# Softmax one unit deeper in the attention slots, four gate chunks moved into slots 0 to 7, the weight fold cut into half-steps

## The reference

```python
def adaln_params(c, w, b):
    mod = jax.nn.silu(c) @ w + b            # shift, scale, gate
def attention_branch(h, ...):
    q, k, v, g = jnp.split(h @ w_in, ...)
    q = partial_rope(rms_norm(q, q_norm_g), positions)
    k = partial_rope(rms_norm(k, k_norm_g), positions)
    o = banded_sink_attention(q, k, v, sinks)   # window 128, softmax with a sink per head
    return (o * jax.nn.silu(g)) @ w_out
def pool_branch(h, ...):
    v, g = jnp.split(h @ w_in, [POOL_WIDTH], axis=-1)
    mixed = einsum('bsgc,gcd->bsgd', multiscale_pool(v), w_group) * scale
    return (mixed * jax.nn.silu(g)) @ w_out
for i in range(2):
    h = rms_norm(x, norm_g[i]) * (1.0 + scale) + shift
    x = x + gate * branch
```

## Time and profile before

| | before |
|---|---|
| median of 3 runs | 1516.83 us |
| the profiled execution | 1514.76 us |
| its span | 1513.0 us |
| PE busy | 1427.6 us, 94% of the span |
| PE's weight loads busy | 1206.2 us, 80% |
| DVE, ACT, POOL busy | 890.8, 537.3, 385.7 us |
| longest total wait of PE | 28.7 us, in the first stage |
| the next | 28.2 us in 16 waits, at_tr waiting for at_pr |

### The profile page before, as it was taken

How to read it: one execution, slowest core, us unless ns; L and a number is a source line. 1 busy time by engine, 2 the same in 40 slices (tenths; PEclk the granted TensorE clock), 3 DMA queues, 4 the chain that set the end, 5 groups by cost and what they waited for, 6 DMA issues and landing times.

```text
span 1513.0 us, 20206 instructions
## 1 busy us (share of the span) xinstructions
PE 1427.6 (94%) x7240; PEld 1206.2 (80%) x7240; DVE 890.8 (59%) x1524; ACT 537.3 (36%) x1270; POOL 385.7 (25%) x551
## 2 busy tenths in 40 slices
PE   1899999999999987799999999999999999999999
PEld 1678878788778876788888888788888888888887
DVE  7777666665444447777777775625555543555522
ACT  2443443333211126675555563322222212222200
POOL 2333333321222214455555554310000100000000
PEclk9999999999999998999999999999999999999999
DMA  8655555434899776756776765831121562112142
GB/s 311 219 183 194 192 186 199 176 138 169 336 345 366 282 296 229 252 216 217 287 274 236 283 256 202 299 98 54 45 76 49 169 193 72 47 42 77 50 153 84
DMA packets 96787, 285.62 MB, mean 189 GB/s; under 512 B 10768, under 2 KB 40496, under 8 KB 87088
## 3 DMA queue, kind: packets, MB, share of 16 engines
q1 hardware_dynamic: 87760, 250.74, 46.2%
q0 software_dynamic: 8928, 33.59, 6.4%
HBM read 196.22 MB, written 88.08 MB: 188 GB/s over the span
## 4 chain that ended last, share of the span: by engine, by line
PE 72%; DVE 9%; DMA 8%; ACT 5%; issue 3%; POOL 2%; SPq 1%; ACTq 0%; DVEq 0%; POOLq 0%
PE po_f_ps L1839 23%; PE po_y_ps L1855 12%; PE at_y_ps L1411 10%; PE ga_g_ps L929 8%; PE qk_proj L663 7%; PE at_o_ps L1395 5%; PE at_s_ps L1367 3%; DMA values_split<-qk_late 3%; DMA ga_ada<-in_ada_w 2%; PE at_tr L1377 2%; ACT at_pr L1187 1%; DMA ga_raw<-in_attn_w_gate 1%; DMA po_xn<-x_mid_t 1%; POOL qk_rq L306 1%; PE qk_tr L679 1%
## 5 line engine op out<-in xcount | busy, mean ns | idle before, releaser
L1839 PE MATMUL po_f_ps<-po_ht,po_w 128*128 128x512 f32 x1536 | 349.0, 389 | 0.0
L1839 PEld LDWEIGHTS po_f_ps<-po_ht,po_w 128*128 128x128 f32 x1536 | 288.2, 188 | 60.1 <-DVE po_ht L1701 0.3
L663 PE MATMUL qk_proj<-qk_w_qkv,qk_ht 128*128 128x512 f32 x1152 | 280.3, 399 | 7.0 <-DVE qk_w_qkv L539 4.0
L663 PEld LDWEIGHTS qk_proj<-qk_w_qkv,qk_ht 128*128 128x128 f32 x1152 | 214.9, 190 | 54.0 <-issue 6.1
L1411 PE MATMUL at_y_ps<-at_zt,at_w 128*128 128x512 f32 x768 | 198.4, 400 | 3.1 <-DVE at_x L1300 3.1
L1855 PE MATMUL po_y_ps<-po_zt,po_w 128*128 128x512 f32 x768 | 174.7, 389 | 0.0
L1855 PEld LDWEIGHTS po_y_ps<-po_zt,po_w 128*128 128x128 f32 x768 | 144.1, 188 | 29.9
L1411 PEld LDWEIGHTS at_y_ps<-at_zt,at_w 128*128 128x128 f32 x768 | 138.4, 190 | 28.7 <-issue 4.1
L1688 DVE TENSOR_TENSOR po_w<-po_raw,po_w 128x1024 fp32r<-128x1024 f32 x48 | 58.8, 1225 | 128.6 <-ACT po_w L1622 128.6
L1143 POOL TENSOR_SCALAR_AFFINE_SELECT at_pt<-at_ph 128x512 fp32r<-128x512 f32 x128 | 83.3, 674 | 188.6 <-ACT at_ph L1194 188.6
L306 POOL TENSOR_TENSOR qk_rq<-qk_mq,qk_half 128x8 f32<-128x8 f32 (+1 forms) x48 | 70.3, 1464 | 177.8 <-DVE qk_mq L485 177.7
(11 more groups left out here) (168 smaller groups left out, 1956.4 us busy)
## 6 DMA issues: line engine op xcount, KB each, us to landing
at_w<-out_weight_split SPq DMA_DIRECT2D x32, 1024.0 KB, 6.2
queries_t<-qk_late SPq DMA_DIRECT2D x16, 1024.0 KB, 4.0
ga_ada<-in_ada_w POOLq DMA_DIRECT2D x64, 256.0 KB, 4.9
at_qt<-queries_t SPq DMA_DIRECT2D x16, 1024.0 KB, 8.0
ht_split<-qk_ht SPq DMA_DIRECT2D x6, 2048.0 KB, 9.6
values_split<-qk_late SPq DMA_DIRECT2D x16, 768.0 KB, 4.5
at_vs<-values_split SPq DMA_DIRECT2D x16, 768.0 KB, 4.9
qk_late<-in_ada_w SPq DMA_DIRECT2D x16, 512.0 KB, 6.1
```

Source lines behind the costliest of these rows:

```text
L663: last = nc.tensor.matmul(proj[:, b * BANK:(b + 1) * BANK], ht[:, s % 2, m, k, t * P:(t + 1) * P], w_qkv[:, w, k, b * BANK:(b + 1) * BANK] ...
L1839: last = nc.tensor.matmul(f_ps[:, bank(j, h), :], w[:, i % 2, a, k, :], ht[:, h, m, k, :], start=(n == 0), stop=(n == 3 * KC - 1))
```

## The change

Three things are changed.

**Softmax one unit deeper.** In slot i PE now does p_round(i-2) and values(i-3), ACT does exps(i-1) ahead of `z_hi`, `p_hi(i-2)` comes behind it, and POOL masks unit i-2. `BEHIND` goes from 3 to 4, and the first output chunk from slot 19 to slot 20.

**Four gate chunks.** The dense part of the gate stage ends after 28 chunks. The last four (`FILL`) are done in slots 0 to 7 of the attention stage, 12 matmuls in each slot, on one PSUM bank (`FILL_BANK`); chunk n waits for the silu of chunk n-1. The last six pieces of the modulation sum move into slots 0 to 5, the last `sum_mods` to slot 7 and `set_mods` to slot 8. The pieces of the output weight begin at gate chunk 6 instead of 8.

**The fold.** It becomes 32 half-steps of 6 matmuls. Two go into each of the slots 9 to 19, behind the transposes; the other ten go in pairs into the second slot of output chunks 0 to 4. A half-step's load is 128 KB into one of two buffers, asked for one slot before ACT reads it. The folded pieces are evicted and stored singly.

```diff
@@ gate stage @@
+    FILL = KC // 2
+    DENSE = SLOTS - FILL
+    FIRST_BANKS, RING_BANKS, FILL_BANK = (6, 0, 1, 2), (6, 3, 4, 5), 6
     def g_bank(q):
-        return g_ps[:, (q + 2) % 4, :]
+        if q >= DENSE:
+            return g_ps[:, FILL_BANK, :]
+        return g_ps[:, FIRST_BANKS[q] if q < 4 else RING_BANKS[q % 4], :]
     def out_piece(q):
-        return (q - KC) // 3 if q >= KC and (q - KC) % 3 == 0 and (q - KC) // 3 < KC else None
+        return (q - 6) // 3 if q >= 6 and q % 3 == 0 and q < DENSE else None
+    def fill_product(pe, n, ks):
+        q, f = DENSE + n, FILL + n
+        if ks[0] == 0:
+            pe.wait_ge(silu_done, q if n > 0 else DENSE - 3)
+        for k in ks:
+            for w, m in PRODUCTS:
+                last = nc.tensor.matmul(g_bank(q), split_of(f, w)[:, k * P:(k + 1) * P], ht[(NSB - 2) % 2][:, m, k, :],
                                        start=(k == 0 and (w, m) == PRODUCTS[0]), stop=(k == KC - 1 and (w, m) == PRODUCTS[-1]))
...
@@ attention stage: places @@
-    BEHIND = 3
+    BEHIND = 4
+    FILL, FILL_SLOTS = ga["fill"], HALVES * ga["fill"]
+    FOLD_FROM = FILL_SLOTS + 1
+    def fold_slot(v):
+        return FOLD_FROM + v // 2 if v // 2 < EARLY else first_slot(v // 2 - EARLY) + HALVES - 1
+    def folds_in(i):
+        return [v for v in range(FOLDS) if fold_slot(v) == i]
...
@@ SP @@
-    def load_fold(sp, u):
-        wait(sp, fold_lo, u - 2)
-        sp.dma_start(wv_raw[:, u % 3], wvt[GC * f:GC * (f + 1)][:, :, pair * ROWS:(pair + 1) * ROWS].rearrange("c p n -> p c n")).then_inc(fold_loaded[u % 3], 16)
+    def load_fold(sp, v):
+        if v == 0:
+            sp.wait_ge(ga["g_done"], ga["slots"])
+            sp.wait_ge(weights["lo"], ga["items"])
+        if v >= 2:
+            sp.wait_ge(fold_lo, wv_split(v - 2))
+        sp.dma_start(wv_raw[:, v % 2], wvt[GC * f:GC * (f + 1)][:, :, b * P:(b + 1) * P].rearrange("c p n -> p c n")).then_inc(fold_loaded[v % 2], 16)
...
-            if i + 3 < FOLDS:
-                load_fold(sp, i + 3)
-            if i in (4, 5, 6):
-                load_w(sp, i - 4)
-                load_x(sp, i - 4)
+            for v in folds_in(i - 1):
+                store_fold(sp, v)
+            for v in folds_in(i + 2):
+                load_fold(sp, v)
+            if i in range(FILL_SLOTS + 1, FILL_SLOTS + 4):
+                load_w(sp, i - FILL_SLOTS - 1)
+                load_x(sp, i - FILL_SLOTS - 1)
...
@@ ACT @@
             if i < UNITS:
                 previous(i)
-            if 0 <= i - 3 < FOLDS:
-                fold_evict(i - 3)
+            if 1 <= i <= UNITS:
+                exps(i - 1)
             if 0 <= i - BEHIND < UNITS:
                 z_hi(i - BEHIND)
-            if 1 <= i <= UNITS:
-                p_hi(i - 1)
-            if i < UNITS:
-                exps(i)
-            if i < FOLDS:
-                fold_high(i)
+            if 2 <= i <= UNITS + 1:
+                p_hi(i - 2)
+            for v in folds_in(i):
+                fold_evict(v)
+            for v in folds_in(i + 1):
+                fold_high(v)
...
@@ PE @@
-            if 0 <= i - 2 < FOLDS:
-                fold(i - 2, 0)
+            fill(i, 0)
             for c, k in part:
                 output(c, list(range(k, k + quarter)))
-            if 1 <= i <= UNITS:
-                p_round(i - 1)
-            if 0 <= i - 2 < FOLDS:
-                fold(i - 2, 1)
+            if 2 <= i <= UNITS + 1:
+                p_round(i - 2)
+            for v in folds_in(i):
+                fold(v)
+            fill(i, 1)
...
-            if 2 <= i <= UNITS + 1:
-                values(i - 2)
+            if 3 <= i <= UNITS + 2:
+                values(i - 3)
```

More of the change, by code:

```diff
@@ L861, in lo, with load_ada @@
         nc.vector.tensor_tensor(split_of(i, LO), raw[:, (RING0 + i) % RAW], split_of(i, HI).bitcast(F32), ALU.subtract).then_inc(w_lo, 1)
-    def scalar(act):
[L864 to L872, removed]
+    def load_ada(pool, n):
+        layer, col = JOBS[n // KC]
+        wait(pool, ada_added, n - 3)
+        pool.dma_start(ada[:, n % 4, :], ada_w[layer][n % KC * P:(n % KC + 1) * P, col:col + BANK]).then_inc(ada_loaded[n % 4], 16)
@@ new lines, in tanh, with silu @@
+    def tanh(act, q):
+        act.wait_ge(g_done, q + 1)
+        if q % KC == 0:
+            wait(act, sg_stored, 16 * (q // KC))
+        nc.scalar.activation(sg[:, :, q % KC, :], g_bank(q).rearrange("p (n t) -> p n t", n=PER), ACT.Tanh,
+                             scale=0.5).then_inc(tanh_done, 1)
+    def silu(dve, q):
+        dve.wait_ge(tanh_done, q + 1)
+        nc.vector.scalar_tensor_tensor(sg[:, :, q % KC, :], sg[:, :, q % KC, :], 1.0, g_bank(q).rearrange("p (n t) -> p n t", n=PER),
+                                       ALU.add, ALU.mult).then_inc(silu_done, 1)
@@ new lines, in sum_mods @@
+    def sum_mods(pe, j):
+        if j == 0:
+            pe.wait_ge(consts_set, 1)
+            pe.wait_ge(qk["hx_done"], KC * NB // 2)
+        pe.wait_ge(ada_added, KC * (j + 1))
+        for c in range(PER):
+            last = nc.tensor.matmul(mod_ps[:, j * PER + c:j * PER + c + 1], sums[:, j % 2, c * P:(c + 1) * P],
+                                    ones[:, 0:1], start=True, stop=True)
+        last.then_inc(mod_summed, 1)
+    def fill_product(pe, n, ks):
[5 more added lines that the diff above has]
+                last = nc.tensor.matmul(g_bank(q), split_of(f, w)[:, k * P:(k + 1) * P], ht[(NSB - 2) % 2][:, m, k, :],
+                                        start=(k == 0 and (w, m) == PRODUCTS[0]), stop=(k == KC - 1 and (w, m) == PRODUCTS[-1]))
+        if ks[-1] == KC - 1:
+            last.then_inc(g_done, 1)
@@ L873, in scalar @@
+    def scalar(act):
+        for q in range(DENSE):
+            tanh(act, q)
             if q < KC // 2:
@@ L878, in vector @@
     def vector(dve):
[L879 to L906, removed]
+        for q in range(DENSE):
             for n in range(ada_by(q - 1), ada_by(q)):
-                add_ada(n)
-            silu(q)
+                add_ada(dve, n)
+            silu(dve, q)
             if q < KC // 2:
@@ L931, in gate_chunk @@
             last.then_inc(g_done, 1)
-        def sum_mods(j):
-            if j == 0:
-                pe.wait_ge(consts_set, 1)
-                pe.wait_ge(qk["act_ev"], 2 * NB)
-            pe.wait_ge(ada_added, KC * (j + 1))
-            for c in range(PER):
-                last = nc.tensor.matmul(mod_ps[:, j * PER + c:j * PER + c + 1], sums[:, j % 2, c * P:(c + 1) * P],
-                                        ones[:, 0:1], start=True, stop=True)
-            last.then_inc(mod_summed, 1)
-        for q in range(SLOTS):
+        for q in range(DENSE):
             gate_chunk(q)
```

287 lines of the change are left out of this document (177 added, 110 removed).

## The result

| | before | after |
|---|---|---|
| median, same chip | 1516.16 us (4 runs) | 1533.05 us (4 runs) |
| the profiled execution's span | 1513.0 us | 1533.3 us |
| PE busy | 1427.6 us | 1431.2 us |

The ratio is 1.0099, 95% interval 1.0076 to 1.0123: the change makes the kernel 1% slower. The forecast was 1506 us in a range of 1491 to 1516.

A forecast was written before the change was run, and what follows sets the result against it. PE was taken as the bound, losing 37.4 us to waits or slow clock in the fold's stretch; 3.0 + 5.0 + 9.2 + 0.8 + 9.5 = 27.5 us lost instead, 9.9 less, giving 1506 us, range 1491 to 1516.

The forecast's parts named there:

- Slots 10 to 19, the loads: Fold loads land late behind chunk and block loads, holding ACT's split, then DVE and PE: 10.3 us lost.
- the third: Rival: in slots 9 to 19 every pair waits for its load at ACT's split; up to 1538 us, chance 0.09.
- the 10.3 less a little: Late-load term as entered in the sum, 9.5 us, since a late slot leaves the queue emptier for the next.
- The ring opens with the depth: Divided probabilities get a whole slot more; the transposes' 27.4 us of waits fall under 5 us.
- Slots 0 to 7: Gate chunks wait for the silu before, about 1.5 us at slot 2, and Tanh for staging: 3.0 us lost.
- Slots 8 and 9: First fold load waits for the last gate matmul, second pair's queues behind 2.75 MB: 5.0 us, bounds 1 and 9.
- Slots 10 to 19: Slots of 5.2 us lose 9.2 us over ten; late fold loads add 0.8 and 9.5 us.
- Elsewhere: Gate stage taken at 0, bounds 4 us growth or 1 less; five of slots 20 to 29 get 1.44 us more PE work.
- The long slots: Two slots, at 13 to 14 and 17 to 18, 4 us or more longer, behind loads of 8 us and more.
- The first rival's rule: About 2.0 us per DMA plus bytes at 436 GB/s, so fold loads aren't late; rival at 1492 us, chance 0.25.

The follow-up runs named there:

- e4: The kernel before with only the softmax one unit deeper, gate chunks and fold as before: 1505.47 us, ratio 0.9898 to the kernel before.
- e11: The kernel of e10 with the softmax back at the old depth, gate chunks and half-steps left moved: 1514.12 us, ratio 0.9964 to the kernel before.
- e7: The changed kernel with the output weight's pieces split behind gate chunks 6, 9, 12, 15, 18, 20, 22 and 25: 1537.32 us, ratio 1.0127.
- e5: The changed kernel with four staging buffers for folded pieces and their stores asked for one turn earlier, ahead of the big loads: 1513.39 us, ratio 0.996.
- e10: The changed kernel with big loads spread over more turns, four staging buffers, and fold loads and stores last in SP's turn: 1500.69 us, ratio 0.9885.
- e8: The changed kernel with folded pieces' stores from POOL's queue, four staging buffers and the output weight's pieces earlier: 1516.55 us, ratio 0.9989.
- e6: The changed kernel with the folded pieces' stores asked for by POOL on its own queue, two staging buffers kept: 1525.09 us, ratio 1.0047.

## Why the prediction was wrong

**The step that failed** is "Slots 10 to 19, the loads". It put 0.8 + 9.5 us on late fold loads and nothing on stores. In the changed kernel the loads of these slots landed in time, but for one pair that ACT waited 3.1 us for. The stores, last in the turn and with two buffers, held ACT for 37.0 us. PE waited 28.9 us in slots 11, 12, 13 and 17 by that (4.5, 3.1, 11.8 and 9.5). With what ran at slow clock behind the waits, these four slots took 54.6 us for 17.1 us of work. The prediction followed one transfer of the new two-deep ring and not the other. The price was about right (8.4 us said behind a block's loads and 8.2 measured, 9.5 said behind 4 MB and 11.3 measured), the transfer that paid it was wrong. And with the stores late, SP's next load is asked for late too, and finds its queue empty.

Of the rivals the third came nearest, 1538 us against 1533. It had the place (the split on ACT) and a two-deep ring, but named loads, and each slot instead of four. That its time is so near is luck: it charged ten slots with 5.1 us each, and four were late by 37.4 us. Its chance of 0.09 rested on the 2.7 us of a load on an empty queue; the stores at the end of SP's turn start behind a chunk's or a block's loads.

The sum has a slip of its own: "the 10.3 less a little" isn't 9.5, for 0.8 + 9.5 is the 10.3 in full. It moves nothing here.

**Point by point.**
- *The ring opens with the depth*: right. The 27.4 us fell to 0, and 3.9 us of waits for at_pl took their place. The five slots in which ACT waits 1.3 us or less for a DMA (14 to 16, 18 and 19) take 4.3, 4.7, 5.7, 4.3 and 5.3 us, where 5.2 was said. e4 and e11 show the gain twice, 15 and 13.4 us.
- *Slots 0 to 7*: 3.0 us said, 7.8 measured. Slot 2 waits 3.6 us and not 1.5, behind the store of the output weight's seventh piece (10.30 us to landing). e7 shows that this can't be cured by moving the piece.
- *Slots 8 and 9*: 5.0 said, 2.9 measured, inside the bounds.
- *Slots 10 to 19*: 9.2 + 0.8 + 9.5 = 19.5 said, 42.8 measured. This is 23.3 of the 30.2 us that the sum was off (from 9.9 less to 20.3 more); the other points here make 5.9, and 1.0 stays unassigned.
- *Elsewhere*: the gate stage was set at 0 with a bound of +4. It lost 3.2 us, just over the 3 that the prediction named as a sign of being wrong: two waits (3.1 us at the modulation instead of the 2.27 of the earlier trace rows, 1.1 at w_fill) and a stretch of slower clock behind them. The stretch behind chunk 0 grew by 6.8 us, about its half-steps, as said.
- *The long slots*: two were forecast, at 13 to 14 and 17 to 18, behind loads. Slots 13 and 17 are the longest (18.0 and 16.5 us), behind stores, and slots 11 and 12 are long too (11.0 and 9.1).
- *The first rival's rule*: in slots 11 to 19 the loads did not come late, so far right. The time did not follow, since a second transfer had the same deadline, and e5 shows loads late once it is met.

What stays open: which of the gate stage's transfers costs the 3.2 us and the rest of slots 0 to 7. The output weight's pieces, the silu's store and the block's first loads meet there, and e7 only exchanged one for another. Nor was a kernel run with the gate chunks between the units and the fold as before, so the shares of the two moved parts are not separated. And e10 joins three edits: whether the order and the four buffers would do without the spread wasn't run.

## What to carry to other kernels

When a change makes a ring shallower or moves it to a tighter slot, price every transfer that touches it: the store that frees a buffer as well as the load that fills it. Read from the issuing engine's timeline what stands ahead of each in the same turn and the turn before. A wait can hide another: a cure of one late transfer let the next one show (e5, e8), and what helped was slack, order and a lower peak together (e10). Of a change with several parts, run the part that removes the measured wait by itself first: here it held the whole gain.

## What the runs showed of the hardware

A second queue evened out the landings of small stores beside big loads and gave them no lane of their own. From POOL's queue, asked for 3 us or less behind big loads, they took 6.3 to 7.2 us, beside 1.25 MB as beside 4 (e6), and could land before a load asked for earlier. From SP's queue they landed behind all that stood ahead: 5.4 to 6.0 us behind 1.25 MB, 8.2 behind 2.75, 11.1 to 11.3 behind 4. With nothing ahead they took 2.1 to 2.6.

The division on DVE got cheaper with its new place in the slot. Between 700 and 900 us it took 1107 ns; now, behind the copy and the reduction of the next scores, it takes 705 ns for the same shape:

```profile
L1352 DVE TENSOR_TENSOR at_pr<-at_pr,at_rden 128x512 f32<-128x512 f32 x35 | 24.7, 705 | 1.2
```

It goes with the order and not with the moved parts: 692 ns in e4 (the depth alone) and 1082 in e11 (all but the depth). The 1107 is a mean of two kinds. Before the change 19 of the 35 divisions took 0.69 us and 16 took 1.6, and each of the 16 began while POOL was in its addition to at_acc:

```profile
806.32 1.29 POOL L1152 TENSOR_TENSOR at_acc<-at_acc,at_sqx 128x512 f32<-128x512 f32 x1
...
806.56 1.60 DVE L1271 TENSOR_TENSOR at_pr<-at_pr,at_rden 128x512 f32<-128x512 f32 x1
```

None of the 19 did. That this addition is the cause is read from such meetings; no run moved it alone.
